# The eighth block of squares of each norm is added on GpSimd, and the norm's sums are asked for some product steps later

## The chip, the cores and the metric

The kernel runs on one core of one Trainium2 chip. The metric is the device time of one execution in microseconds (us); lower is better. Each kernel is run several times and the median is taken. A change of 0.2%, about 5 us here, is the least that a measurement of this kernel can tell from no change.

## What is computed

A two-layer trunk with one latent stream `h` (512 tokens) and one context stream `hc` (256 tokens), 1024 features each, all in fp32. Each layer has three stages, and each stage begins with an RMS norm over the features, scaled and shifted by vectors made from a conditioning input:

```python
def rms_norm(x, g):
    y = x * lax.rsqrt(jnp.mean(x * x, axis=-1, keepdims=True) + NORM_EPS)
    return y * g

def modulate(x, shift, scale):
    return x * (1 + scale) + shift

# one layer (the context does the same with its own shift, scale and gate)
h = h + 0.5 * g1 * swiglu(modulate(rms_norm(h, g_ffn1), s1, sc1), w1_gate, w1_up, w1_down)   # d_ff = 2816
h = h + g2 * mixer(modulate(rms_norm(h, g_mix), s2, sc2) @ w_in) @ w_out                     # attention and Fourier
h = h + 0.5 * g3 * swiglu(modulate(rms_norm(h, g_ffn2), s3, sc3), w2_gate, w2_up, w2_down)
# after both layers
out = rms_norm(h, g_final)
```

In the last layer the context is no longer needed behind the mixer's keys and values, so the mixer's output and the last feed-forward stage work on the 512 latent tokens alone.

## The kernel before

**Layout.** Features lie on the 128 partitions, in KD = 8 blocks (numbered d or k, 0 to 7); tokens lie along the free axis. Latent and context tokens stand side by side, 768 columns in all (`TOK`), or 512 (`SEQ`) once only the latent ones are left. Every fp32 operand of a product is split in a high and a low fp32r part (`xh`, `xl` for the activations, `whi`, `wlo` for the weights: ScalarE rounds the high part, VectorE subtracts it to get the low one), and each product step is three matmuls: high by high, low by high, high by low.

**Stages.** There are six: ffn1, mix, ffn2 of layer 0 and of layer 1, numbered n = 0 to 5; n = 6 is the final norm. The boundary before stage n is called boundary n here. At boundaries 1 to 4 the outgoing stage is 768 columns wide, at 5 and 6 it is 512.

**How a stage ends.** `last_products` (TensorE) makes the last output blocks (d = 2 to 7 behind a feed-forward stage, 4 to 7 behind the mixer) in two rounds: first all of them for the first part of the columns (512, or 256 when only 512 are left), then all of them for the second part (256 columns). As soon as a block is done VectorE adds it to `h`: `early_residual` in the first round (line 1609), `late_residual` in the second (line 1617). ScalarE squares the new block (`square`, line 980) into one of the two buffers of `sq`, and GpSimd adds the squares into `acc` (`sum_squares`, lines 704 and 707), blocks 0 to 6 only. Inside the second round TensorE runs `sum_chunks(n, width, 0)`: for each tile of 128 tokens one matmul with `acc` as weights and a column of ones as moving data (line 2078), and one with block 7's squares, accumulated into the same PSUM column (line 2079). Then ScalarE takes the root (line 986), VectorE inverts it (1533) and widens it (1560), and TensorE turns it into a row for all partitions (`spread_rstd`, line 2087), again between product steps of the second round. The arguments `at_sum` and `at_spread` of `last_products` are the (block, step) before which the two stand.

**How a stage begins.** `norm` on VectorE multiplies `h` by scale and root, block by block (`t_lat`, line 1585), ScalarE adds the shift and rounds (`xh`, 1048), VectorE makes the low part (`xl`, 1592). First come the eight blocks of the first part of the columns, then those of the second part (`t_ctx`, or `t_lat` again). Between blocks 5 and 6 of the first part both queues hold the second part's root: ScalarE `std(n, width, 1)` and `widen`, VectorE `invert(n, width, 1)`. Both wait for the sums of the second part. On TensorE `product_pair` begins two products at once, in 16 steps on the first part (u is the product, k the block: (0,0), (0,1), (0,2), (0,3), (1,0), (0,4), (1,1), (0,5), (1,2), (0,6), (1,3), (0,7), (1,4) ...), where step (0,k) waits for block k of `xl`, and then 16 steps on the second part. It runs `sum_chunks(n, width, 1)` ahead of step number 3 and `spread_rstd(n, width, 1)` ahead of step number 8. The second part of `norm` waits for that spread. At a feed-forward stage ScalarE, paced by VectorE's blocks of the second part, also adds the shift to all of `t_lat` and `t_ctx` (line 1007), and only then runs `plain_silu(0)` (line 866), for which TensorE's next product (`pe.wait_ge(silu_done, p0 + 1)` in `pe_ffn`) waits.

**What sets the order.** Every engine's order is written out by hand, each engine runs its queue in order, and counting semaphores join them. In the last feed-forward group VectorE's queue has, for each output block d, first the splits of weights two blocks ahead (`ahead`, line 1481), then `early_residual(s, d)`. TensorE has two PSUM rings, so the first-round product of block d waits for the residual of block d - 2.

## Time and profile before

| | |
|---|---|
| median of 3 runs | 2569.25 us (2569.17 to 2571.13) |
| profiled execution's own time | 2568.64 us |
| its span | 2566.9 us, mean granted TensorE clock 0.994 |
| TensorE matmul busy | 2504.4 us (98%) |
| VectorE / ScalarE / GpSimd busy | 1911.5 (74%) / 1155.0 (45%) / 731.1 us (28%) |

The 1.7 us between span and time lie around the profiled instructions. A busy share of matmuls counts pipelined ones and says that TensorE seldom stands still, not that it is at its peak. In the timelines a row is: start, length, engine, line, operation, output <- input, shape, count, and in brackets the idle time ahead of it and what ended it. Lengths overlap by about 0.1 us where instructions follow each other.

### The profile page before, as it was taken

To read this page: it belongs to the slowest core of one execution; us is meant where nothing else is said; L and a number is where in the kernel's file an instruction comes from. 1 tells how busy PE (TensorE), PEld (TensorE's weight loads), DVE (VectorE), ACT (ScalarE), POOL (GpSimd) and SP (SyncE) were. 2 spreads that over 40 slices of the span, in tenths; PEclk is the share of its full clock that TensorE was granted. 3 is DMA by queue.
4 is the path that set the end of the run, shared out by engine and by line. 5 is a ranking of instruction groups with operands and counts; after the bars stand their busy time and mean duration, and the time that the engine had idled before them with its cause. 6 is when DMAs were issued, how large, how long until landed. Compare 5 with 4: busy or idle time off the path is not lost. (4 is left out here: it accounts for less than half of the span.)

```text
span 2566.9 us, 40418 instructions
## 1 busy us (share of the span) xinstructions
PE 2504.4 (98%) x14978; PEld 2309.3 (90%) x14978; DVE 1911.5 (74%) x3244; ACT 1155.0 (45%) x2202; POOL 731.1 (28%) x654
## 2 busy tenths in 40 slices
PE   7999999999999999999999999999999999999998
PEld 4999999988888889999999899999998888899997
DVE  5888788765488588888755888888557596877775
ACT  5523433443387362433434624334344485644444
POOL 1322221223166231221131322212312264333332
PEclk8999999999999999999999999999999999999999
DMA  6344444214430124444312244453122531133332
GB/s 248 101 144 142 133 136 144 83 58 147 126 84 8 59 86 136 131 140 148 115 50 83 75 139 128 132 154 122 57 74 95 145 79 50 62 102 102 105 100 79
DMA packets 132003, 276.18 MB, mean 108 GB/s; under 512 B 15584, under 2 KB 35296, under 8 KB 130528
## 3 DMA queue, kind: packets, MB, share of 16 engines
q1 hardware_dynamic: 131808, 273.60, 34.5%
q8 instruction: 120, 1.97, 0.3%
q14 instruction: 75, 0.61, 0.1%
HBM read 260.43 MB, written 13.11 MB: 107 GB/s over the span
## 5 line engine op out<-in xcount | busy, mean ns | idle before, releaser
L1481 DVE TENSOR_TENSOR wlo<-raw,whi 128x512 fp32r<-128x512 f32 (+2 forms) x672 | 492.3, 743 | 308.7 <-ACT whi L974 307.2
L974 ACT ACTIVATE whi<-raw 128x512 fp32r<-128x512 f32 (+2 forms) x672 | 399.6, 605 | 381.8 <-PE ring L1993 232.5
L1888 PE MATMUL ring<-xh,whi 128*128 128x384 f32 (+1 forms) x1280 | 413.7, 323 | 9.7 <-DVE rstd L1460 5.2
L1888 PE MATMUL ring<-xl,whi 128*128 128x384 f32 (+1 forms) x1280 | 412.1, 322 | 0.0
L1888 PE MATMUL ring<-xh,wlo 128*128 128x384 f32 (+1 forms) x1280 | 411.9, 322 | 0.0
L1888 PE MATMUL ring<-th,whi 128*128 128x384 f32 (+1 forms) x960 | 312.0, 325 | 2.7 <-DVE wlo L1481 1.9
L1888 PE MATMUL ring<-th,wlo 128*128 128x384 f32 (+1 forms) x960 | 311.3, 324 | 0.0
L1888 PE MATMUL ring<-tl,whi 128*128 128x384 f32 (+1 forms) x960 | 311.1, 324 | 0.0
L655 POOL TENSOR_TENSOR raw<-raw,s_two 128x512 f32<-128x512 f32 x80 | 123.2, 1539 | 627.3 <-DVE wlo L1481 581.4
L1488 DVE SCALAR_TENSOR_TENSOR ada_junk<-ada_tile,row 128x1024 bf16<-128x1024 f32 x256 | 301.4, 1214 | 0.0
L641 POOL TENSOR_TENSOR s_one<-raw 128x512 f32<-128x512 f32 x80 | 105.6, 1319 | 549.8 <-DMA raw<-w_gu 429.8
L1888 PEld LDWEIGHTS ring<-xh,whi 128*128 128x128 f32 x1280 | 241.3, 189 | 13.6 <-DVE rstd L1460 7.2
L1888 PEld LDWEIGHTS ring<-xl,whi 128*128 128x128 f32 x1280 | 241.4, 189 | 0.7
L1888 PEld LDWEIGHTS ring<-xh,wlo 128*128 128x128 f32 x1280 | 241.4, 189 | 0.0
L1601 DVE SCALAR_TENSOR_TENSOR h<-ring,vec_gate,h 128x512 f32<-128x512 f32 x250 | 149.2, 632 | 73.7 <-PE ring L1993 49.4
L1993 PE MATMUL ring<-act_hi,wlo 128*128 128x512 f32 (+1 forms) x714 | 197.1, 345 | 0.0
L1993 PE MATMUL ring<-act_hi,whi 128*128 128x512 f32 (+1 forms) x714 | 196.9, 345 | 0.0
L1993 PE MATMUL ring<-act_lo,whi 128*128 128x256 f32 (+1 forms) x714 | 196.7, 345 | 0.0
L1888 PEld LDWEIGHTS ring<-th,whi 128*128 128x128 f32 x960 | 180.8, 188 | 3.9 <-issue 1.8
L1888 PEld LDWEIGHTS ring<-tl,whi 128*128 128x128 f32 x960 | 180.7, 188 | 0.0
L1888 PEld LDWEIGHTS ring<-th,wlo 128*128 128x128 f32 x960 | 180.5, 188 | 0.0
L950 ACT ACTIVATE acc<-acc 128x768 f32<-128x768 f32 (+1 forms) x80 | 63.5, 794 | 173.0 <-DVE acc L1466 173.0
(217 smaller groups left out, 5487.4 us busy)
## 6 DMA issues: line engine op xcount, KB each, us to landing
raw<-w_gu SPq DMA_DIRECT2D x352, 256.0 KB, 3.1
ada_tile<-w_turned SPq DMA_DIRECT2D x130, 512.0 KB, 3.7
raw<-w_down SPq DMA_DIRECT2D x96, 256.0 KB, 3.5
raw<-w_down SPq DMA_DIRECT2D x64, 192.0 KB, 2.5
raw<-w_in SPq DMA_DIRECT2D x48, 256.0 KB, 3.4
raw<-w_down SPq DMA_DIRECT2D x64, 128.0 KB, 2.1
raw<-w_out SPq DMA_DIRECT2D x32, 256.0 KB, 7.9
ada_first<-w_first SPq DMA_DIRECT2D x4, 1536.0 KB, 13.5
```

What stands on the lines that cost most here:

```text
L641: pool.tensor_tensor(s_one[:], raw[:, a21 % RAWS], raw[:, a22 % RAWS], ALU.add).then_inc(s_done, 1)
L655: pool.tensor_tensor(raw[:, a11 % RAWS], raw[:, a12 % RAWS], s_two[:], ALU.subtract).then_inc(s_done, 1)
L950: act.activation(c1[:, 0:width], c1[:, 0:width], ACT.Silu).then_inc(silu_done, 1)
L974: act.activation(weights(q, 0, cols)[0], src[:, 0:cols], ACT.Copy).then_inc(whi_ready, 1)
L1481: dve.tensor_tensor(w_l, src[:, 0:cols], w_h.bitcast(F32), ALU.subtract).then_inc(wlo_ready, 1)
L1488: dve.scalar_tensor_tensor(out=junk[:, c], in0=tile, scalar=1.0, in1=rows[:, c], op0=ALU.mult, op1=ALU.mult, accum_out=modv[:, c, i:i + 1] ...
L1601: last = dve.scalar_tensor_tensor(out=h[:, d, a:b], in0=ring[slot][:, a:b], scalar=vec_gate[:, c, d:d + 1], in1=h[:, d, a:b], op0=ALU.mult ...
L1888: last = pe.matmul(out, w, x, start=(start and k == 0 and m == 0), stop=(k == HALF - 1 and m == 2), skip_group_check=not start)
L1993: last = pe.matmul(out[:, a:b], w, x[:, k, a:b], start=(k == 0 and m == 0), stop=(k == parts[-1][1] - 1 and m == 2))
```

## The change

Three edits. First, GpSimd's `sum_squares` also adds block 7, and `sum_chunks` at boundaries 1 to 6 has one matmul for each tile of 128 tokens where it had two; the counts of `acc_done` move with it. Boundary 0 keeps its two. Second, the places of `sum_chunks` and `spread_rstd` move back: three steps behind feed-forward stages and in `product_pair` (also at boundary 0), two and three steps behind the mixer. Third, in the last stage (`width == SEQ`) `early_residual` stands ahead of that block's weight splits in VectorE's queue.

```diff
@@ -111,7 +111,7 @@
                          whole=whole_tiles(kind), parts=parts, squares=squares, sums=sums_of)
                 parts += KD - s["whole"]
                 squares += 2 * KD - s["whole"]
-                sums_of += 2 * (KD - 1) - s["whole"]
+                sums_of += 2 * KD - s["whole"]
                 self.stages.append(s)
                 if kind == "mix":
                     s["tile"] = []
@@ -438,7 +438,7 @@
         def sum_count(s, d, p):
 
 
-            return s["sums"] + d + 1 + (KD - 1 - s["whole"] if p == 1 and d >= s["whole"] else 0)
+            return s["sums"] + d + 1 + (KD - s["whole"] if p == 1 and d >= s["whole"] else 0)
 
         def rounds_late(s):
 
@@ -696,7 +696,7 @@
 
                 width, whole = s["out_width"], s["whole"]
                 steps = [(d, 0, (0, width)) for d in range(whole)]
-                steps += [(d, p, halves(width)[p][0:2]) for p in range(2) for d in range(whole, KD - 1)]
+                steps += [(d, p, halves(width)[p][0:2]) for p in range(2) for d in range(whole, KD)]
                 for d, p, (a, b) in steps:
                     pool.wait_ge(sq_done, square_count(s, d, p))
                     if d == 0:
@@ -1413,6 +1413,9 @@
                     g, d = unit
                     if open_pair is not None:
                         product_rest(open_pair)
+                    part_first = width == SEQ and g == GROUPS - 1 and d >= s["whole"]
+                    if part_first:
+                        early_residual(s, d)
                     for e in range(len(plan.parts(g))):
                         ahead(s["down"][unit] + e)
                     if open_pair is not None:
@@ -1423,7 +1426,8 @@
                         one_gate(n, layer, stage, d)
                         dve.wait_ge(gate_ready, KD * n + d + 1)
                     if g == GROUPS - 1 and d >= s["whole"]:
-                        early_residual(s, d)
+                        if not part_first:
+                            early_residual(s, d)
                     else:
                         residual(s["down"][unit] + len(plan.parts(g)), d, down_ring(g, d), width)
                     if n == 0 and unit == (GROUPS - 1, 0):
@@ -1867,7 +1871,7 @@
             for d in range(2, s["whole"]):
                 slot_free(pe, s, out_r + d)
                 product(ring[out_ring(s, d)], out_at[d], WHOLE_TILE, xh, xl, s["out_width"])
-            last_products(s, out_at, WHOLE_TILE, xh, xl, (s["whole"], 5), (s["whole"] + 1, 2))
+            last_products(s, out_at, WHOLE_TILE, xh, xl, (s["whole"], 7), (s["whole"] + 1, 5))
 
         def pe_ffn(pe, s, product, part_product, product_pair, last_products):
 
@@ -1975,7 +1979,7 @@
                     pe.wait_ge(resid_done, s["resid"] + KD * g + d - 1)
                     product(ring[down_ring(g, d)], s["down"][g, d], plan.parts(g), act_hi, act_lo, width)
             at = s["whole"]
-            last_products(s, [s["down"][GROUPS - 1, d] for d in range(KD)], plan.parts(GROUPS - 1), act_hi, act_lo, (at + 1, 0), (at + 2, 0))
+            last_products(s, [s["down"][GROUPS - 1, d] for d in range(KD)], plan.parts(GROUPS - 1), act_hi, act_lo, (at + 1, 3), (at + 2, 3))
 
         @block.tensor
         def _(pe):
@@ -2044,9 +2048,9 @@
                     if k + 4 < KD:
                         order.append((0, k + 4))
                 for i, (u, k) in enumerate(order):
-                    if i == 3:
+                    if i == 6:
                         sum_chunks(n, width, 1)
-                    if i == 8:
+                    if i == 11:
                         spread_rstd(n, width, 1)
                     if k == 0 and n > 0:
                         pe.wait_ge(resid_done, s["resid"] - 1 + u)
@@ -2067,16 +2071,16 @@
             def sum_chunks(n, width, p):
 
                 a, b, o, _ = halves(width)[p]
-                last_sq = (sq[:, (KD - 1) % 2, a:b] if n > 0 else sq_lat[:, (KD - 1) % 2] if p == 0 else sq_ctx[:, KD - 1])
+                last_sq = sq_lat[:, (KD - 1) % 2] if p == 0 else sq_ctx[:, KD - 1]
                 if n == 0:
                     pe.wait_ge(acc_first[p], KD - 1 - p)
                     pe.wait_ge(sq_first[p], KD)
                 else:
-                    pe.wait_ge(acc_done, sum_count(stages[n - 1], KD - 2, p))
-                    pe.wait_ge(sq_done, square_count(stages[n - 1], KD - 1, p))
+                    pe.wait_ge(acc_done, sum_count(stages[n - 1], KD - 1, p))
                 for i, m in enumerate(range(a // P, b // P)):
-                    pe.matmul(side[:, o + i:o + i + 1], acc[:, m * P:(m + 1) * P], ones[:, 0:1], start=True, stop=False)
-                    last = pe.matmul(side[:, o + i:o + i + 1], last_sq[:, i * P:(i + 1) * P], ones[:, 0:1], start=False, stop=True)
+                    last = pe.matmul(side[:, o + i:o + i + 1], acc[:, m * P:(m + 1) * P], ones[:, 0:1], start=True, stop=n > 0)
+                    if n == 0:
+                        last = pe.matmul(side[:, o + i:o + i + 1], last_sq[:, i * P:(i + 1) * P], ones[:, 0:1], start=False, stop=True)
                 last.then_inc(ssq_ready, 1)
 
             def spread_rstd(n, width, p):
```

## Rows read from the trace of the kernel before

**Rows 1.** The page, busy time of the engines.
```profile
PE 2504.4 (98%) x14978; PEld 2309.3 (90%) x14978; DVE 1911.5 (74%) x3244; ACT 1155.0 (45%) x2202; POOL 731.1 (28%) x654
```
**Rows 2.** TensorE's waits: line, releaser, us in total, times, longest.
```profile
PE row L2078 <- ACT sq L980: 4.4, 4, 1.1
```
**Rows 3.** Timeline of TensorE at boundary 1.
```profile
552.53 0.32 PE L2078 MATMUL row<-ones,acc 128*128 128x1 f32 x2
552.94 0.36 PE L2078 MATMUL row<-ones,acc 128*128 128x1 f32 x2
...
556.16 0.60 PE L2087 MATMUL row<-ident,rstd 128*128 128x128 f32 x4
...
567.47 0.35 PE L2078 MATMUL row<-ones,acc 128*128 128x1 f32 x2 [1.12 <-ACT sq L980]
...
571.89 0.38 PE L2087 MATMUL row<-ident,rstd 128*128 128x128 f32 x2
```
**Rows 4.** Timeline of VectorE at boundary 1.
```profile
556.79 1.41 DVE L1585 SCALAR_TENSOR_TENSOR t_lat<-h,vec_scale,row 128x512 f32<-128x512 f32 x2
...
560.11 1.24 DVE L1592 SCALAR_TENSOR_TENSOR xl<-t_lat,modv,xh 128x512 fp32r<-128x512 f32 x1
...
567.46 0.74 DVE L1592 SCALAR_TENSOR_TENSOR xl<-t_lat,modv,xh 128x512 fp32r<-128x512 f32 x1
...
568.91 0.73 DVE L1585 SCALAR_TENSOR_TENSOR t_lat<-h,vec_scale,row 128x512 f32<-128x512 f32 x1
569.56 0.74 DVE L1592 SCALAR_TENSOR_TENSOR xl<-t_lat,modv,xh 128x512 fp32r<-128x512 f32 x1
...
572.42 0.87 DVE L1585 SCALAR_TENSOR_TENSOR t_ctx<-h,vec_scale,row 128x256 f32<-128x256 f32 x2
```
**Rows 5.** Timelines of ScalarE and GpSimd at boundary 1: squares and adds.
```profile
551.73 0.63 ACT L980 ACTIVATE sq<-h 128x512 f32<-128x512 f32 x1 [2.77 <-DVE h L1609]
...
566.91 0.42 ACT L980 ACTIVATE sq<-h 128x256 f32<-128x256 f32 x1 [0.33 <-DVE h L1617]
...
549.04 1.29 POOL L707 TENSOR_TENSOR acc<-acc,sq 128x512 f32<-128x512 f32 x1 [0.39 <-ACT sq L980]
...
560.07 0.74 POOL L707 TENSOR_TENSOR acc<-acc,sq 128x256 f32<-128x256 f32 x1 [1.96 <-ACT sq L980]
```
**Rows 6.** Timelines at boundary 2, into a feed-forward stage: TensorE, VectorE, ScalarE.
```profile
904.32 0.38 PE L2087 MATMUL row<-ident,rstd 128*128 128x128 f32 x2
...
915.78 0.52 PE L1993 MATMUL ring<-xh,whi 128*128 128x512 f32 x2
...
904.84 0.87 DVE L1585 SCALAR_TENSOR_TENSOR t_ctx<-h,vec_scale,row 128x256 f32<-128x256 f32 x2
...
914.54 0.81 ACT L866 ACTIVATE acc<-ring 128x768 f32<-128x768 f32 x1 [0.35 <-PE ring L2004]
```
**Rows 7.** Windows at boundaries 0 and 3: length, busy (x) by engine, PEclk, DMA.
```profile
48.00:60.00 12.00, 12.00 (x54) 10.04 (x55) 10.72 (x23) 9.72 (x19) 0.00 (x0) 0.87 0.07 23
...
1420.00:1423.50 3.50, 3.50 (x10) 2.72 (x10) 3.14 (x6) 2.65 (x6) 0.00 (x0) 0.53 0.02 5
```
**Rows 8.** Timeline of TensorE: the second spread at boundaries 0, 3 and 5.
```profile
53.11 0.38 PE L2087 MATMUL row<-ident,rstd 128*128 128x128 f32 x2
...
1424.88 0.38 PE L2087 MATMUL row<-ident,rstd 128*128 128x128 f32 x2
...
2194.68 0.38 PE L2087 MATMUL row<-ident,rstd 128*128 128x128 f32 x2
```
**Rows 9.** Timelines of VectorE and TensorE in the last stage's first round.
```profile
2533.32 1.67 DVE L1481 TENSOR_TENSOR late_ffn<-raw,late_ffn 128x384 fp32r<-128x384 f32 x2 [1.11 <-ACT late_ffn L974]
2534.91 0.47 DVE L1609 SCALAR_TENSOR_TENSOR h<-ring,vec_gate,h 128x256 f32<-128x256 f32 x1
...
2535.44 0.39 PE L2004 MATMUL ring<-act_hi,late_ffn 128*128 128x256 f32 x1 [1.10 <-DVE h L1609]
...
2542.68 0.39 PE L2004 MATMUL ring<-act_hi,late_ffn 128*128 128x256 f32 x1 [0.36 <-DVE h L1609]
```

## The prediction

> **What bounds the kernel now.** I read the page first: TensorE's matmuls fill 98% of the span [rows 1], so only three things can move the end: work taken off TensorE, one of its few waits removed, or a new wait. The table of waits names the one the change aims at: four times TensorE stands 1.1 us ahead of the second part's sums, on ScalarE's last square [rows 2]. The timelines show where: at boundary 1 the sums could begin at 566.35 and begin at 567.47 [rows 3], since block 7's square starts only at 566.91 [rows 5]. The same pattern stands at boundaries 3 and 4 (851.4 and 1370.3 us later, to 0.01 us) and in the final norm. Then I read VectorE beside it. From 556.79, when the first spread lets the norm begin, its queue is without a gap worth naming until 568.2, and it paces `xh` and `xl`, on which TensorE's 16 paired steps wait one by one [rows 4]. So a boundary is two interleaved queues, not TensorE's alone, and I cost the change by both.
>
> **Work taken off.** A tile's two sums take 552.94 - 552.53 = 0.41, in steady state 0.44 us [rows 3], so one of them is 0.22 us. At boundaries 1 to 4 there are six tiles and at 5 and 6 four: 32 tiles, 7.1 us of TensorE. That is the most this edit can give.
>
> **First sums, boundary 1.** GpSimd's new add of 512 columns takes 1.29 us and starts 0.7 us after its square does; block 7's square starts at 551.73 [rows 5], so `acc` is complete at 553.73. A product step of the second round is 0.36 us (3.63 us from first sum to first spread, less 1.75 for eight sums' pairs and 0.08 to refill, over five steps [rows 3]); three steps later is 553.6, and the sums begin at 553.85. They last 0.88 instead of 1.76. From the first sum to the spread were 3.63 us and are 2.76, so the spread moves from 556.16 to 556.65: 0.49 us *later*, and the norm with it. TensorE would be 0.6 us ahead, but rounds on blocks 6 and 7 wait for residuals in the same queue of VectorE, and that lead is lost. Behind the mixer the sums move only two steps, 0.36 less, which GpSimd's add takes back: the spread is 0.85 later there.
>
> **Second sums, boundary 1.** GpSimd adds block 7's 256 columns: 0.74 us [rows 5]. It starts 0.5 us after the square, at 567.4. VectorE's low part of block 4 starts at 567.46 [rows 4]. Where these two met before, GpSimd at 560.07 and VectorE at 560.11, VectorE took 1.24 instead of 0.74 us [rows 4, 5]. So block 4 is 0.5 us late, and with the 0.49 from above it is ready at 568.20 + 0.99 = 569.19. Step 5 of TensorE, (0,4), waits for it; the sums now stand behind that step. A step on 512 columns is 0.69 us ((571.89 - 567.47 - 0.9 - 0.08)/5 [rows 3]), so the sums begin at 569.9. Before, VectorE's next operation came 1.44 us after the first sum [rows 3, 4]; with half the sums that is 1.0, so 570.9 instead of 568.91. **This is the stall I expect the change to create**: `invert` stands in VectorE's queue ahead of blocks 6 and 7 and of block 5's low part, and it now waits for sums which themselves wait for block 4. Before, they waited for block 2 only and a square. Block 5 is ready at 572.3 instead of 570.3, TensorE waits for it 1.2 us at its step 7, and four steps later, at 575.1, comes the spread that was at 571.89 [rows 3]: 3.2 us later. TensorE at that step is at 575.2 where it was at 574.1: **+1.1 us**. The wait of rows 2 is gone, the halved sums are in, and both are given back. The second part of the norm is 3 us late too, but into the mixer nothing I found waits for its end, so I count nothing for it.
>
> The Trainium skill (SBUF — State Buffer, "SBUF: two separate sides") has the pair of ports that VectorE and GpSimd share as an exclusive lock, held for a whole instruction by whoever starts first, against VectorE operations with two SBUF inputs. The 1.24 us row agrees. By that rule VectorE would lose nothing if it came first, and it misses by some 0.05 us only; the sum would then be 0.5 us less at each of boundaries 1 to 4, 2.0 in all.
>
> **The other boundaries.** At 3, the second spread stood at 1424.88 [rows 8], 1.6 us behind the pattern of boundary 1 (571.89 + 851.4 = 1423.3), because TensorE ran at about half clock, 1.2 of 2.4 GHz, right behind its 1.1 us wait and the sums [rows 7]. Boundary 4 shows the same 1.6 us. The change splits that quiet stretch of 2.0 us in two of 1.2 and 0.5, with a full product between; I take it that the clock then stays up, as it did at boundary 1. So 4 is 1.1 - 1.6 = **-0.5**, and at 3 the spread is 3.2 - 1.6 = 1.6 us later.
>
> Into a feed-forward stage a late spread costs more. ScalarE's `plain_silu(0)` stands behind shifts that are paced by the second part of the norm, and TensorE's next product waits for it. At boundary 2 the silu waited 0.35 us for TensorE at 914.54, ended at 915.35, and TensorE's product began at 915.78 [rows 6]: 0.78 us of slack. The spread (904.32 [rows 6]) comes 3.2 + 0.36 = 3.6 us later, so the product is **+2.8** late. At 3 I take the same slack, so **+0.8**. At 0 nothing is halved and GpSimd adds nothing new, but the steps move: at full clock the spread (53.11 [rows 8]) is 2.3 us later (3.2 less the 0.99 that the add brings), at half clock, which part of the stretch has [rows 7], up to 3.9. Less 0.78 that is 1.5 to 3.1; no row decides, I take the middle, **+2.3**. At 5 the steps are half as long: the spread (2194.68 [rows 8]) is some 1.1 us late, of which ScalarE's table load hides 0.7: **+0.4**.
>
> **Last stage.** In the first round VectorE split weights until 2534.9 and only then did block 2's residual (2534.91), for which TensorE stood 1.10 us, and 0.36 us three more times: each step lasted 2.41 us where its matmuls last 1.8, (2542.68 - 2535.44)/3 [rows 9]. With the residual first, the product on block 4 needs only the split, of which a first half is ready near 2534.7 (the 1.67 us row is 0.83 us of work behind a GpSimd add). So it begins at 2534.7 and block 7's at 2540.1 instead of 2542.68: 2.6 us, between 1.9 if the split meets the next GpSimd add too, and 3.1. In the final norm the sums save 0.45 twice, refilling costs 0.2, and at its end GpSimd's add of 0.74 with 0.1 to start lies on the path. **-2.6 - 0.9 + 0.2 + 0.85 = -2.4.** Nothing hides this last add: behind block 7's square everything waits for it.
>
> **Sum.** 2.3 + 1.1 + 2.8 + 0.8 - 0.5 + 0.4 - 2.4 = +4.5 us. On the profiled execution's own 2568.64 that is 2573.1; the median lies 0.6 above that execution, so the forecast is **2573.7 us**. Its own range is 2570 to 2577: boundary 0 by 0.8 either way, the lock by 2.0 down, the last stage by 0.7, the clock by 1.6 up for each boundary at which it falls after all. Bounds of the new wait are 0 (below) and 1.4 us.
>
> **Rivals.**
> *The lead goes through.* If VectorE's queue has slack where I see none, TensorE keeps 7.1 us of sums, 4 x 1.1 us of waits less the 0.85 of the last add, 3.2 us of half clock and 2.6 us in the last stage: 16.5 us, 2552.8. For it: TensorE is 98% busy. Against: the 1.1 us waits are on a chain that VectorE paces, and the moved sums make that queue wait for TensorE. Chance 0.12.
> *The silu is not reached.* If shifts and silu have more slack than boundary 2's 0.78 us, TensorE's own places count: 1.0 instead of 2.8 at boundary 2, -0.4 at 3, 0 to 1.8 at 0. That is 4 to 5 us less, 2569. Chance 0.10.
> *The clock falls (other side).* Place: the wait for block 5 at step 7, behind step 5, the sums and one more product, five times. Price: 1.6 us each, as at boundaries 3 and 4. It decides from the point where two short waits count like one of 2 us: then 2573.7 + 5 x 1.6 = 2581.7, or 2575 to 2580 where it happens at some. Chance 0.15.
> *The edit in the last stage does nothing*, since the splits, not the residual, end the wait and are then last at TensorE. +2.6, 2576. Against: a block's split (0.83) and residual (0.47) add up to 1.3 us, under 1.8. Chance 0.08.
>
> **How the numbers follow.** The forecast has 0.55, of which 0.18 lies beyond 2574.4, where slower by over 0.2% begins (0.2% is what a measurement can tell). Slower: 0.18 + 0.15 + 0.08 = 0.41. Faster (under 2564.1): 0.12. Same: 0.37 + 0.10 = 0.47. The range leaves out the first rival and the far half of the third: 2565 to 2579.
>
> **What would show it.** Right: TensorE's waits on line 2078 are gone except in the final norm, where they are about 1.9 us; new waits of about 1.2 us on `xl`, line 1592, stand at step 7 of the pair, and VectorE's wait on the root (ahead of line 1533) is 1 us longer; `t_ctx` at boundary 1 starts 3 us later against the first sum; the silu's release, line 866, holds TensorE's product at 0, 2 and 3. In the last stage the four waits on line 1609 are gone and the last block starts 2.6 us sooner. Wrong: if VectorE's wait ahead of 1533 stays at 0.6 us, or product 1 does not wait for the silu. A granted clock of about 0.5 in other places than now would move each boundary by 1.6 us.

## The result, and the profile after

The changed kernel takes 2578.09 us (median of 5 runs, 2576.97 to 2582.04), the kernel before 2569.17 us beside it. The ratio is 1.0044, with an interval of [1.0033, 1.0055]: slower, by 8.9 us in the medians (the interval is 8.5 to 14.1 us), where +4.5 was forecast. The wide range of 2565 to 2579 us just holds it; the forecast's own, 2570 to 2577, does not.

The profiled execution of the changed kernel took 2582.04 us, the highest of the five, with a span of 2580.2 us; that of before took 2568.64. So of the 13.4 us between the two profiles about 4 belong to this one execution, which has to be kept in mind wherever a shift is read below.

The page of the changed kernel, busy time of the engines:

```profile
PE 2500.7 (97%) x14914; PEld 2299.3 (89%) x14914; DVE 1921.5 (74%) x3244; ACT 1154.3 (45%) x2202; POOL 741.0 (29%) x666
```

Against [rows 1], TensorE has 64 matmul records less, and GpSimd 12 additions and 9.9 us more, as the change says. VectorE has the same 3244 instructions and yet 10.0 us more busy time. That is the first hint, since the change gives it no new work.

TensorE's waits in the changed kernel (line, releaser; us in total, times, longest), the lines on which it differs:

```profile
PE ring L2008 <- DVE xl L1596: 13.7, 18, 2.7
PE ring L1892 <- DVE rstd L1464: 7.6, 9, 2.4
PE ring L1892 <- issue: 6.7, 4, 2.0
PE ring L1997 <- ACT acc L866: 3.0, 4, 0.9
PE row L2081 <- POOL acc L707: 2.2, 2, 1.8
```

and the same view of the kernel before, where all of these lines lie four lower:

```profile
PE ring L1888 <- DVE rstd L1460: 5.2, 8, 1.2
PE ring L1888 <- issue: 4.1, 4, 2.0
PE ring L2004 <- DVE xl L1592: 3.1, 3, 2.7
PE ring L2004 <- DVE h L1609: 2.2, 4, 1.1
PE ring L1993 <- ACT acc L866: 0.4, 1, 0.4
```

The wait of [rows 2] (4.4 us on ScalarE's square) is gone, and so is the 2.2 us on line 1609 (the last stage). In their place stand 10.6 us more on `xl`, 2.6 on the silu, 2.6 on "issue" and 2.4 on `rstd`, and nine short waits on residuals, 1.9 us in all. To place them, each product matmul of the one trace was set beside the same matmul of the other; the table gives by how much the changed kernel lags at the start and at the end of each place.

| place | lag, us | gained | forecast |
|---|---|---|---|
| start, boundary 0, FFN start | 0.53 to 4.64 | +4.1 | +2.3 |
| boundary 1 | 4.65 to 5.99 | +1.3 | +1.1 |
| boundary 2 to the silu's product | 6.24 to 8.99 | +2.75 | +2.8 |
| rest of that stage | 8.99 to 8.49 | -0.5 | 0 |
| boundary 3 and FFN start | 8.49 to 11.69 | +3.2 | +0.8 |
| boundary 4 | 11.69 to 11.50 | -0.2 | -0.5 |
| boundary 5 and FFN start | 11.53 to 12.49 | +1.0 | +0.4 |
| last stage, shortly ahead of its last output products | 12.81 to 16.01 | +3.2 | 0 |
| last output products and start of the final norm | 16.01 to 13.05 | -3.0 | -2.4 with the next row |
| end of the final norm | 13.05 to 13.3 | +0.3 | |

### The stall that was forecast

Boundary 1 of the changed kernel, TensorE's timeline: a wait of 0.65 us for block 4 ahead of the second sums, a wait of 1.05 us for block 5, and the second spread.

```profile
573.88 0.47 PE L2008 MATMUL ring<-xh,whi 128*128 128x512 f32 x1 [0.65 <-DVE xl L1596]
...
574.66 0.50 PE L2081 MATMUL row<-ones,acc 128*128 128x1 f32 x4
...
577.02 0.49 PE L2008 MATMUL ring<-xh,whi 128*128 128x512 f32 x1 [1.05 <-DVE xl L1596]
...
579.89 0.38 PE L2091 MATMUL row<-ident,rstd 128*128 128x128 f32 x2
```

VectorE and GpSimd beside it:

```profile
572.50 1.24 DVE L1596 SCALAR_TENSOR_TENSOR xl<-t_lat,modv,xh 128x512 fp32r<-128x512 f32 x1
...
575.49 0.17 DVE L1537 RECIPROCAL rms_inv<-rms 128x2 f32<-128x2 f32 x1 [1.75 <-ACT rms L986]
...
576.22 0.75 DVE L1596 SCALAR_TENSOR_TENSOR xl<-t_lat,modv,xh 128x512 fp32r<-128x512 f32 x1
...
572.45 0.74 POOL L707 TENSOR_TENSOR acc<-acc,sq 128x256 f32<-128x256 f32 x1 [1.64 <-ACT sq L980]
```

Each step of the forecast is here. GpSimd's addition starts 0.05 us ahead of VectorE's low part of block 4, which takes 1.24 instead of the 0.74 us of [rows 4]. VectorE then stands 1.75 us ahead of the inversion, where it stood 0.63 before, and block 5's low part behind it keeps TensorE 1.05 us (forecast 1.2). The same pair, 0.65 and 1.05, stands at boundaries 2, 3 and 4. Over the whole trace 11 of VectorE's 40 low parts on 512 columns take over 1.1 us where 7 did: one more at each of boundaries 1 to 4.

The Trainium skill (SBUF — State Buffer, "SBUF: two separate sides") has a lock held by whichever of VectorE and GpSimd starts first. Here the trace agrees: GpSimd started at 572.45 and VectorE at 572.50, when GpSimd had 0.69 us left, and VectorE pays 0.50 us.

### The silu

At boundary 2 the spread comes late and the silu with it, TensorE's timeline:

```profile
914.22 0.38 PE L2091 MATMUL row<-ident,rstd 128*128 128x128 f32 x2
...
924.64 0.62 PE L1997 MATMUL ring<-xh,whi 128*128 128x512 f32 x2 [0.85 <-ACT acc L866]
```

TensorE's product waits 0.85 us for the silu, as at boundaries 0 and 3 (the fourth case is the 0.4 us that was there before).

### The clock

At boundaries 3 and 4 of the kernel before the granted clock fell [rows 7, 8]. In the changed kernel two windows around the same places (length, busy by engine, then granted clock, DMA share, GB/s) show it at 1.00:

```profile
1424.00:1430.00 6.00, 5.04 (x22) 3.46 (x21) 4.96 (x8) 2.40 (x5) 2.01 (x2) 1.00 0.28 87
1946.00:1952.00 6.00, 5.01 (x21) 3.38 (x20) 5.09 (x8) 2.53 (x5) 2.02 (x2) 1.00 0.00 0
```

So the clock stays up where the quiet stretch is split, as forecast, and the rival of a falling clock did not come true at these boundaries. That the splitting keeps it up is not shown: with the last-stage edit alone (below) the waits of 1.09 us stand unsplit at both boundaries, and the clock stays up all the same.

### What nobody had on the list

Two of the gained lags have no step in the forecast. The first stands behind the silu, at a split of weights in VectorE's queue. VectorE's and GpSimd's timelines at the start of the feed-forward stage behind boundary 2, first of the changed kernel:

```profile
942.61 1.75 DVE L1485 TENSOR_TENSOR wlo<-raw,whi 128x512 fp32r<-128x512 f32 x1
...
942.53 1.29 POOL L646 TENSOR_TENSOR s_two<-s_one,raw 128x512 f32<-128x512 f32 x1
```

and of the kernel before:

```profile
933.66 1.03 DVE L1481 TENSOR_TENSOR wlo<-raw,whi 128x512 fp32r<-128x512 f32 x1
...
932.85 1.29 POOL L646 TENSOR_TENSOR s_two<-s_one,raw 128x512 f32<-128x512 f32 x1
```

Before, GpSimd had run 0.81 of its 1.29 us when VectorE's split came. Now GpSimd, whose sums follow VectorE's earlier splits, is 9.68 us later than before, and VectorE, which waits for TensorE's product ahead of this split, only 8.95: they meet when GpSimd has run 0.08 us. The split takes 1.75 instead of 1.03 us. From there on VectorE runs without a gap in both traces, so the 0.7 us go through to its line 1464 (1460 before), at whose end TensorE's product 13 us on begins. It waits 1.58 instead of 0.85 us, although the profile puts the wait down to "issue":

```profile
955.83 0.41 PE L1892 MATMUL ring<-xh,whi 128*128 128x384 f32 x1 [1.58 <-issue]
```

The lag grows by 0.9 there at boundaries 0 and 3. Secondly, shortly ahead of the last output products of the last stage, VectorE's split of `s_one` (0.67 us before) met GpSimd's line 655 at 2524.36:

```profile
2524.45 1.72 DVE L1485 TENSOR_TENSOR wlo<-s_one,whi 128x512 fp32r<-128x512 f32 x1
...
2526.56 0.39 PE L1892 MATMUL ring<-xh,whi 128*128 128x256 f32 x1 [2.43 <-DVE rstd L1464]
```

The collision is the end of a longer chain. GpSimd's sums of this group wait for a load of weights; the same row in the kernel before and in the changed one:

```profile
2503.37 1.29 POOL L641 TENSOR_TENSOR s_one<-raw 128x512 f32<-128x512 f32 x1 [1.53 <-DMA raw<-w_gu]
...
2517.75 1.29 POOL L641 TENSOR_TENSOR s_one<-raw 128x512 f32<-128x512 f32 x1 [3.10 <-DMA raw<-w_gu]
```

The loads were issued 12.8 us later than before, as late as TensorE is, but the row starts 14.4 us later. So GpSimd's three sums lie beside three splits of VectorE that take 4.96 us together where they took 2.65, and VectorE is late for the collision above too. Behind the wait of 2.43 us TensorE's clock fell, in the window

```profile
2528.00:2531.50 3.50, 3.50 (x19) 3.50 (x18) 1.96 (x4) 1.76 (x5) 0.00 (x0) 0.52 0.03 7
```

which is 1.5 of the 3.2 us by which the lag grows over this stretch; the longer wait is 1.9, less 0.2 us gained just ahead of it. In the profiles of all twelve other kernels, below, the same wait is 0.5 to 1.4 us, the clock stays up and the lag grows by 0 to 0.7. It goes with the start of GpSimd's row: 5.1 us ahead of a given matmul in the kernel before and in five of the twelve, with a wait of 0.5 us; 4.0 to 4.3 us ahead in the other seven, with 1.2 to 1.4; 3.4 us ahead in the changed kernel, with 2.4.

Over the whole trace 172 of VectorE's 832 splits take over 0.9 us where 160 did, 8.8 us more in all; with 1.9 us more for the low parts that is what the page's 10.0 us of busy time consist of, within 0.7.

### The profile page after: what moved, and what is told of

Its sections match the earlier page's. It is cut to its first block and busy times, and to the rows that moved or that the text cites. A ratio compares the mean times of both kernels' runs of the same rounds, so it can differ in the third digit from the quotient of the medians.

```text
span 2580.2 us, 40298 instructions
## 1 busy us (share of the span) xinstructions
PE 2500.7 (97%) x14914; PEld 2299.3 (89%) x14914; DVE 1921.5 (74%) x3244; ACT 1154.3 (45%) x2202; POOL 741.0 (29%) x666
## 5 line engine op out<-in xcount | busy, mean ns | idle before, releaser
L1485 DVE TENSOR_TENSOR wlo<-raw,whi 128x512 fp32r<-128x512 f32 (+2 forms) x672 | 501.3, 756 | 304.4 <-ACT whi L974 303.0
```

The costliest lines, as they stand in the source:

```text
L1485: dve.tensor_tensor(w_l, src[:, 0:cols], w_h.bitcast(F32), ALU.subtract).then_inc(wlo_ready, 1)
```

## The experiments

All kernels compute the full result. Times are medians; each group ran on one chip beside the kernel before, whose median is given. VectorE's wait ahead of `rms_inv`, the inversion, is 8.2 us in all in the kernel before and 15.7 in the changed one.

### Group 1: each edit alone, and the inversion moved

**The last-stage edit alone** on the kernel before:

```diff
+                    part_first = width == SEQ and g == GROUPS - 1 and d >= s["whole"]
+                    if part_first:
+                        early_residual(s, d)
                     for e in range(len(plan.parts(g))):
                         ahead(s["down"][unit] + e)
```

> The kernel before with the third edit alone: in the last stage each first-round residual stands ahead of that block's weight splits in VectorE's queue. Theory (the residual was queued behind splits that it does not need): TensorE's four waits on line 1609 in the last stage (1.10 and 3 x 0.36 us) go, the last block of the first round starts 2.6 us sooner, and the kernel is 2.6 us faster (1.9 to 3.1), ratio 0.9990. Rival (the splits end the wait anyway): the waits move to the splits' line and the time is unchanged, within 0.5 us.

Measured: 2565.08 against 2569.85, ratio 0.9982 [0.9974, 0.9991]. Across the last output products the lag goes from -3.2 to -5.7: -2.5 us, as forecast (2.6). The median says -4.8, and the interval reaches from 2.3 to 6.7 us; its profile also has no drop of the clock at boundaries 3 and 4 (-1.6 us at each), where nothing was edited. The block's residual now goes ahead of its split, VectorE's timeline:

```profile
2532.28 0.47 DVE L1613 SCALAR_TENSOR_TENSOR h<-ring,vec_gate,h 128x256 f32<-128x256 f32 x1
2532.67 0.88 DVE L1485 TENSOR_TENSOR late_ffn<-raw,late_ffn 128x384 fp32r<-128x384 f32 x2
```

**GpSimd's eighth block alone**, with the places of before (the first hunks of the change, `sum_chunks` included):

```diff
-                steps += [(d, p, halves(width)[p][0:2]) for p in range(2) for d in range(whole, KD - 1)]
+                steps += [(d, p, halves(width)[p][0:2]) for p in range(2) for d in range(whole, KD)]
```

> The kernel before with the first edit alone: GpSimd adds block 7 and TensorE sums one tile, at the old places, so the sums wait for GpSimd. Theory (the moved places are what costs): the wait ahead of the second part's sums grows from 1.1 to about 2.2 us at boundaries 1, 3 and 4 and the sums themselves save 0.45, so each boundary is 0.5 to 0.9 us later, the end of the final norm 0.4 us later; in all +2 to +4 us, and up to 1.6 us more for each boundary at which the longer wait brings the clock down. Rival (GpSimd's add, by its own length and by the shared ports, is the cost of the whole change): +8 us or more, as the whole change.

Measured: 2575.79, ratio 1.0026 [1.0015, 1.0036]: +5.9, above the 2 to 4 without the clock. TensorE's waits:

```profile
PE row L2077 <- POOL acc L707: 13.0, 10, 1.8
```

13.0 us of waits for GpSimd stand where 4.4 us for ScalarE stood. What the edit saves on TensorE (7 us) it loses at the same line. The profiled execution, 2571.82, is the fastest of the eight and only 3.2 us above the kernel before's, so this trace shows half of the +5.9; the rest is not placed. Neither is it the clock behind the long waits, in this trace: two windows at boundary 3, the first behind the 1.07 us wait ahead of the first sums, the second behind the 1.71 us wait ahead of the second,

```profile
1406.00:1410.00 4.00, 4.00 (x24) 4.00 (x25) 2.67 (x8) 0.68 (x2) 0.51 (x2) 0.64 0.48 135
...
1421.50:1424.50 3.00, 3.00 (x15) 2.45 (x15) 2.63 (x5) 2.10 (x5) 0.00 (x0) 1.00 0.00 0
```

show it lower behind the shorter wait and at 1.00 behind the longer one, and so it is at boundary 4.

**The places alone** (`last_products` at both calls, sums at step 6, spread at 11), with the sums as before:

```diff
-                    if i == 3:
+                    if i == 6:
                         sum_chunks(n, width, 1)
-                    if i == 8:
+                    if i == 11:
                         spread_rstd(n, width, 1)
```

> The kernel before with the second edit alone: sums and spreads some steps later, TensorE still summing two tiles, GpSimd adding seven blocks. Theory (VectorE's second inversion stands ahead of blocks 5 to 7 in its queue and now waits for sums that stand behind step 5): the wait on block 5 at step 7 of the pair appears at every boundary from 0 to 4 with 1.2 to 1.5 us (the two-tile sums are 0.45 longer), VectorE waits 1.5 us or more ahead of the inversion, and boundary 0 loses the same 4 us as with the whole change. In all +10 us (8 to 13), more than the whole change. Rival (the add is the cost): under +3 us, and no wait at step 7.

Measured: 2584.18, ratio 1.0062 [1.0049, 1.0074]: +14.3, above the upper end of 13. The waits, TensorE's and VectorE's:

```profile
PE ring L2004 <- DVE xl L1592: 11.0, 15, 2.7
PE ring L1993 <- ACT acc L866: 3.0, 4, 0.9
...
DVE rms_inv L1533 <- ACT rms L986: 24.3, 14, 2.2
```

This is the costliest part of the change. The last-stage edit takes 4.8 off it, and on top of the two GpSimd's addition, which costs 5.9 us alone, makes no difference that shows (+9.5 by the sum of the two, +8.9 for the whole change).

**The second inversion behind block 7** in the changed kernel, so that no block stands behind the late sums:

```diff
-                        if p == 0 and d == 6:
+                        if p == 0 and d == KD:
                             invert(n, width, 1)
```

and ScalarE's root and widening behind its eighth block in the same way.

> The changed kernel, with the second part's root moved behind block 7 in both queues: ScalarE takes root and widens after its eighth block, VectorE inverts ahead of its last low part; TensorE's order untouched. Theory (the inversion blocks blocks 5 to 7): the wait on block 5 at step 7 (1.05 us) is gone at boundaries 0 to 4, the second spread is 1.1 to 1.2 us earlier, and the kernel is 5 to 6 us faster than the changed one: about +3 us against before, 2572. Rival (the late spread at step 11 alone sets the loss, or the clock): no more than 1 us off the changed kernel, about +8 against before.

Measured: 2569.44, ratio 1.0004 [0.9995, 1.0013]. Some 9 us are gone, more than the 5 to 6 expected, and with them all of the loss against the kernel before.

```profile
DVE rms_inv L1537 <- ACT rms L986: 8.2, 11, 2.2
...
PE ring L2008 <- DVE xl L1596: 7.2, 12, 2.7
PE ring L1997 <- ACT acc L866: 3.0, 4, 0.9
```

VectorE's wait is back at the 8.2 us of before, and TensorE's waits on `xl` fall by 6.5 us; the silu's do not change. So the forecast's mechanism holds: the *queue behind* the inversion costs most. In the traces the lag across each of boundaries 0 to 5 is 1.0 to 1.4 us less than in the changed kernel, 7.7 us in all. Another 2.5 of the 11 us between the two profiles are the stretch ahead of the last output products, where this kernel's lag grows by 0.7 instead of 3.2 us. What is left are costs too: with its last-stage edit (-4.8 alone) this kernel only equals the one before.

### Group 2: which of the two places

**The spread back at step 8** in the changed kernel, sums still at 6:

```diff
-                    if i == 11:
+                    if i == 8:
                         spread_rstd(n, width, 1)
```

> The changed kernel with the second spread back at step 8 of the pair (the sums stay at step 6, GpSimd's add, the first part's places and the last stage as changed). Theory (two costs: the inversion blocks blocks 5 to 7, and the spread at step 11 holds back the second part of the norm and with it the silu at boundaries 0, 2 and 3): the wait on block 5 at step 7 stays at 1.05 us, TensorE's three waits of 0.85 us on the silu go, the spread comes 2 us sooner, and the kernel is 3 to 5 us faster than the changed one: +4 to +6 against before. Rival (all of the loss is the blocked inversion): within 1 us of the changed kernel, +8.

Measured: 2572.6 against 2568.97, ratio 1.0016 [1.0007, 1.0025], +3.6 where the changed kernel has +8.9.

```profile
DVE rms_inv L1537 <- ACT rms L986: 16.9, 11, 3.9
...
PE ring L2008 <- DVE xl L1596: 13.1, 17, 2.7
PE ring L1892 <- issue: 5.7, 4, 2.0
PE ring L1892 <- DVE rstd L1464: 3.3, 6, 1.3
PE ring L1997 <- ACT acc L866: 0.4, 1, 0.4
```

VectorE stands at the inversion as long as in the changed kernel, but the 2.6 us at the silu are gone, and of the waits inside the feed-forward stages 5.3 us (`rstd` 3.3 instead of 7.6, of which the single 2.43 us is a part, and "issue" 5.7 instead of 6.7).

**The spread at 11 alone** on the kernel before:

```diff
-                    if i == 8:
+                    if i == 11:
                         spread_rstd(n, width, 1)
```

> The kernel before with one number changed: the second spread at step 11 instead of 8. Theory: nothing is lost into the mixer (boundaries 1 and 4), and 1 to 1.5 us at each of boundaries 0, 2 and 3, where the silu waits for the second part of the norm: +3 us (2 to 4.5); VectorE's wait ahead of the inversion stays at 8.2 us in all. Rival (the loss needs both moves, the spread alone lies in slack): within 1 us of before.

Measured: 2573.13, ratio 1.0017 [1.0008, 1.0026]: +4.2, in the expected 2 to 4.5.

```profile
PE ring L1888 <- issue: 6.6, 4, 2.0
PE ring L1993 <- ACT acc L866: 3.0, 4, 0.9
```

Here the two run together without any late sums: 2.6 us at the silu, and 2.5 more at "issue" right behind. There the lag grows by 0.88, 0.69 and 0.91 us at the three starts. A late silu is not needed for this, though. In each of the four kernels with the spread at 11 this wait is 1.5 to 1.6 us at all three starts, against 0.65 to 0.85 before; but it is as long at two of three starts with the sums at 6 alone, with sums at 4 (below) and with sums at 6 and spread at 8 (above), where TensorE waits for no silu at these starts.

**The sums at 6 alone** on the kernel before:

```diff
-                    if i == 3:
+                    if i == 6:
                         sum_chunks(n, width, 1)
```

> The kernel before with one number changed: the second sums at step 6 instead of 3, two tiles each. Theory: TensorE's 1.1 us wait for the square goes, a wait of 1.2 to 1.4 us on block 5 at step 7 comes in its place, and TensorE is about 0.5 us later at boundaries 1 and 2, 1 to 2 us at 0, and up to 1.1 us earlier at 3 and 4, if the clock stays up there: +1 us in all (-1 to +4), VectorE's wait ahead of the inversion 15 us or more. Rival (the inversion is the whole loss of the moved places): +8 us or more.

Measured: 2576.14, ratio 1.0026 [1.0017, 1.0035]: +7.2, well above the expected +1, near the rival's 8.

```profile
DVE rms_inv L1533 <- ACT rms L986: 17.5, 13, 2.5
...
PE ring L2004 <- DVE xl L1592: 10.5, 11, 2.9
```

I had thought that the wait on ScalarE's square, which this edit removes (3.3 us), and two drops of the clock would pay for the new one. They don't: the new waits on `xl` are 7.4 us, and in this trace the clock is up at boundary 4 only (1.00 from 1940 to 1950, but 0.84 from 1420 to 1430). 7.2 and 4.2 add up to 11.4, under the 14.3 of all places moved together; the difference of 2.9 us is the first sums' places or an effect of the two together, and stays open.

**The last-stage edit and sums at step 4** on the kernel before:

```diff
-                    if i == 3:
+                    if i == 4:
                         sum_chunks(n, width, 1)
```

> A version meant to beat both: the kernel before with the residuals ahead of the splits in the last stage and the second sums at step 4 instead of 3, two tiles each, spread at step 8, no new add. Theory: step 3 (0.69 us) fills most of the 1.1 us wait for the square, block 4 is not waited for and the inversion is not later than before, so TensorE gains 0.7 us at boundaries 1, 3 and 4, the clock stays up at 3 and 4 (1.6 us each), and the last stage gives 3 to 5: 8 us faster than before, 2561 (2558 to 2566). Rival (the gain goes as with step 6): as the residual edit alone, 2565.

Measured: 2563.28, ratio 0.9980 [0.9972, 0.9989]. That lies in the expected range of 2558 to 2566, but it can't be told from the last-stage edit alone (0.9982), which was the rival; the step from 3 to 4 brings nothing that shows. The wait on the square is 1.1 us instead of 4.4, those on `xl` 4.7 instead of 3.1.

### Group 3: is the late spread costly by itself, and GpSimd's addition

**Inversion behind block 7, and the spread at 9**, in the changed kernel:

```diff
-                    if i == 11:
+                    if i == 9:
                         spread_rstd(n, width, 1)
```

> The changed kernel with the second root and inversion behind block 7, as in the earlier run of that name (2569.4, ratio 1.0004), and now the second spread at step 9 instead of 11. Full result. Theory (a spread at step 11 is 3 us late for ScalarE's silu, which shows as four TensorE waits of 3.0 us in all, and costs some 4 us however it comes about): 2566, 2564 to 2568.5, silu waits back to 0.4 us in all. Rival (with the root behind block 7 the factors are not there at step 9, and TensorE stands at the spread): waits on rstd ahead of the spread, 2570 or more.

Measured: 2568.93 against 2569.35, ratio 1.0003 [0.9994, 1.0012]. The same as with the spread at 11, where 3 us less were expected: a miss.

```profile
PE row L2091 <- ACT rstd L994: 2.8, 6, 1.3
PE ring L1892 <- issue: 6.5, 4, 2.0
```

The silu waits have left the table, but "issue" stays at 6.5 and TensorE now waits 1.5 us more for the widened factor itself. So moving a step frees one wait and hands part of it to the next, and the rival was right in part.

**The second tile's places back at 3 and 8** in the changed kernel; GpSimd's addition, the later first places and the last-stage edit stay:

```diff
-                    if i == 6:
+                    if i == 3:
                         sum_chunks(n, width, 1)
-                    if i == 11:
+                    if i == 8:
                         spread_rstd(n, width, 1)
```

> The changed kernel with the second tile's sums and spread where they were before, at steps 3 and 8; GpSimd's eighth block, the later first places and the last-stage edit stay. Full result. Theory (the second places are what costs: about 7 for the sums at 6 and 4 for the spread at 11; GpSimd's addition costs only where the sums stand in its way, 1.1 us at a first place and 0.64 at a second): the first places' waits go down to 0.4, the second ones stay at 0.6, the last-stage edit gives its 3 to 4: 2568, 2565 to 2571. Rival (GpSimd's additions cost by themselves, through VectorE's port): 2573 or more, with VectorE's xl waits as in the changed kernel.

Measured: 2572.8, ratio 1.0015 [1.0006, 1.0023]. That is above the expected 2565 to 2571 and just under the rival's 2573, but VectorE's `xl` waits (3.1 us) are those of before, not of the changed kernel, as the rival had them. The later second places cost 5 us within the whole change, and with them undone the kernel is still slower than before. TensorE's waits:

```profile
PE row L2081 <- POOL acc L707: 10.2, 7, 1.8
```

its timeline at boundary 1:

```profile
569.92 0.61 PE L2081 MATMUL row<-ones,acc 128*128 128x1 f32 x4 [1.80 <-POOL acc L707]
```

and a window right behind this wait:

```profile
570.50:573.50 3.00, 3.00 (x11) 2.36 (x11) 2.64 (x5) 2.11 (x5) 0.00 (x0) 0.68 0.00 0
```

At boundaries 1 to 4 each second sum waits 1.7 to 1.8 us for GpSimd, not the 0.6 I had expected from boundary 2 of the run with the addition alone. There the first sums had waited 1.08 us and the second 0.64; now it is 0.38 and 1.72: the wait is the same in all, collected in one place. And in this trace the wait of 1.7 to 1.8 us with the small matmuls behind it is followed by a stretch partly at 1.2 GHz at each of boundaries 1 to 4 (granted clock 0.65 to 0.68 in 3 us), where the kernel before had two such stretches. The addition alone has such waits at boundaries 1, 3 and 4 and keeps the clock at 1.00 behind them. So the addition costs a wait, and in some executions the clock behind it.

**The last-stage edit, sums at 5, spread at 9, inversion behind block 7**, without GpSimd's addition (edits as above, on the kernel before):

```diff
-                    if i == 3:
+                    if i == 5:
                         sum_chunks(n, width, 1)
-                    if i == 8:
+                    if i == 9:
                         spread_rstd(n, width, 1)
```

> The kernel before, with the last-stage edit, the second sums at step 5, the second spread at step 9, and the second root and inversion behind block 7; no addition by GpSimd. Full result. Theory (the later sums are free once no queue of VectorE stands behind them, and a spread at 9 is in time for the silu): 2563, 2560 to 2566, no wait on ACT sq at the second sums and VectorE's wait ahead of the inversion at 8 us or less. Rival (block 5's xl still waits at step 7 or the spread is late): 2567 or more.

Measured: 2564.89, ratio 0.9986 [0.9977, 0.9994], in the expected range of 2560 to 2566.

**The same with sums at 4 and the spread at 8:**

```diff
-                    if i == 3:
+                    if i == 4:
                         sum_chunks(n, width, 1)
```

> As the run before it, but second sums at step 4 and the second spread at step 8, where it was. Full result. Theory (the inversion's place alone, against the run with sums at step 4 and the old place of the inversion, 2563.3): the root comes about 1.5 us later and is still in time, 2562.5, 2560 to 2565. Rival (the factors are late for step 8): TensorE waits on rstd ahead of the spread, 2566 or more.

Measured: 2565.88, ratio 0.9990 [0.9981, 0.9999], above the expected 2560 to 2565. TensorE's waits for the factors (line 2091) rose to 4.5 us from 1.3, as the rival had it.

With sums at 5 the wait ahead of the inversion is down to 6.5 us and in this one to 5.9, under the 8.2 of before, and neither beats the last-stage edit alone. All the gain that these runs find in this change is its last edit.

## Why the forecast was wrong

In medians, against before: last-stage edit -4.8, GpSimd's addition +5.9, places +14.3, together +15.4; the change as a whole +8.9. So the parts together cost 6.5 us less than one by one. Most of that lies between the addition and the places: with the places late, GpSimd is no longer waited for (2.2 us instead of 13.0), while the 7 us of sums stay saved.

- **Boundaries 1 and 2: right**, in mechanism and size (+1.3 for +1.1, +2.75 for +2.8). The inversion's queue, the wait for block 5, the collision of GpSimd's addition with block 4 and the late silu are all in the trace, and moving the inversion took the loss away.
- **The clock at 3 and 4: right in the number, perhaps by luck.** Both drops are gone (-0.2 for -0.5 at boundary 4), but they are gone with the last-stage edit alone too, in which nothing there is changed.
- **The last stage and final norm: right**, -2.7 for -2.4 in the trace, and -2.5 for the edit's -2.6 when it stands alone.
- **Boundary 0: the term was mis-sized.** +4.1 for +2.3. To the silu's product it is 3.1; the remaining 1.0 is the next point. I took boundary 1's 3.2 us over, less 0.99. But in those 3.2 us a wait of 1.1 us for the square goes and the sums get 0.44 us shorter, and at boundary 0 neither is so: the kernel before began its sums at 46.66 without a wait, and they stay as they are. Put back, the two make the lower end of 1.5 into an estimate of 3.0, with no need of the clock. The half-clock stretch stands in both kernels, only elsewhere (granted clock 0.51 from 46.6 to 51.2 before, 0.55 from 53.2 to 57.0 now).
- **Boundaries 0, 3 and 5: the step "a late spread ends at the silu" failed.** I stopped the count at the silu's product. To there it was right at boundary 3 (+0.8) and at 5 (+0.4). What comes behind is a chain of splits for which VectorE and GpSimd take turns, and being late changes where in GpSimd's instruction VectorE's split falls: +0.9 at 0 and at 3, +0.6 at 5. With the spread at 11 alone the same 0.7 to 0.9 appear at three starts. I had counted the new collision with the addition, and not the old ones, whose timing the lateness changes. At 3 another 1.5 us follow at 1493, where TensorE waits 1.16 us for `rstd`. The same step stood behind boundary 2 of the kernel before (1.14 us at 962) and is missing there now, which is how boundary 2 gives its collision back. It moved from 2 to 3 in four of the six kernels with GpSimd's addition and stays at 2 in seven of the eight without; why is open.
- **Ahead of the last output products: no step of mine, +3.2 in the profile.** The other kernels show 0 to 0.7 there. It goes with how late one load of weights landed, and half of it is clock. I take it to belong mostly to the one execution that was profiled, which stands 4 us above the median; there is no second profile to settle that.
- **In the sum**, 4.5 + 1.8 (boundary 0) + 2.4 (boundary 3) + 0.6 (boundary 5) = 9.3: with boundaries 0, 3 and 5 corrected the forecast would have been near the measured +8.9. That it is so near is in part luck, since the terms come from one execution. The whole table without the 3.2 us adds up to +9.6 (0.6 of it between the rows): last stage and final norm are 0.3 better than forecast and the rest of the stage behind boundary 2 gives 0.5 back, while the terms at 1 and 4 are 0.5 worse.
- **The rival "the clock falls"** gave about the right time (2575 to 2580) for the wrong reason: at boundaries 1 to 4 the two short waits with a product between them did not lower the clock, and at 0 the kernel before has a half-clock stretch too.
- **The halved sums** were worth little within the change: they gave TensorE time at a place where it is paced by VectorE. [Rows 4] had said so.

What stays open: why all places together cost 2.9 us more than the two second ones summed, half of what the addition costs alone, and how much of the sizes at boundary 3 would repeat in another execution. No run moved only the first sums' places, and no run parted VectorE's splits from GpSimd's sums. That the collision causes the lag behind the silu is read from the traces, where VectorE runs without a gap from the slower split to the row that TensorE waits for; it was not tested by itself.

## What to carry to other kernels

When a wait is put later in one engine's order, look at what stands *behind* the instruction that waits for it on the other engines: here a reciprocal of 0.17 us in VectorE's queue turned a later sum into 7 us of waits, and putting that reciprocal behind the blocks that don't need it gave some 9 us back. Move the consumer with the producer, or don't move the producer. And don't end the count of a delay at the first instruction it reaches: where two engines block each other, a lag that goes into a stage comes out of it changed.

## What the hardware showed that I had not expected

- **Who comes second pays what the first has left.** VectorE's split took 1.03 us when GpSimd had started 0.81 us ahead of it and 1.75 us when 0.08 us ahead; ahead of the last output products 1.72 for 0.67 us. This holds over the whole of both traces. A split of 512 columns takes 0.67 to 0.70 us where GpSimd has nothing under way. Where one starts inside an instruction of GpSimd that has 0.2 us or more left, it takes 0.67 plus what is left less 0.12 us, within 0.03, in 346 of 358 cases; the other twelve lie in GpSimd rows of over 7 us and take 0.68, and what those rows hold is open. Where VectorE's split starts first it keeps its 0.68 us and GpSimd is the longer one (1.59 instead of 1.29 us when 0.43 us of the split were left). So 0.05 us in who starts can move 0.5 us from one engine to the other. Of some 10 us that VectorE was busier, 8.8 lie in splits, of which the change adds none.
- **Whether the clock falls behind a short wait is not a matter of that wait alone.** Behind 1.7 to 1.8 us and the sums it fell at all four boundaries with the second places undone (granted clock 0.65 to 0.68 in the 3 us behind), and at none of the three (1.00) with GpSimd's addition alone, where it fell behind the 1.1 us ahead of the first sums of boundaries 3 and 4 (0.64 and 0.60). Behind 1.1 us it fell at boundaries 3 and 4 of the kernel before and not at 1; with the last-stage edit alone, which touches none of them, at none of the three; with the spread at 11 alone at 1 and 4. Behind two waits of 0.65 and 1.05 us with a product and the sums between, it fell at none of the boundaries 1 to 4 of the changed kernel, and it did fall behind the single wait of 2.4 us near the end of the last stage (0.52). No length of wait in these runs tells the two cases apart.
- **One profile is worth less than it seems.** At the first product, up to which the kernels are all but the same, they stand from 0.3 us ahead of the kernel before to 2.1 us behind it. A load that landed 1.6 us later, as ahead of the last output products, went with 3 us of difference at the end.
